# One decoder step on one core: weight passes in whole-row slabs over eight PSUM banks, residual by an identity product, cache pages over 8 partitions

## What is computed

```
mix = jnp.concatenate([rmsnorm(mla_o, w["norm_mla_out"]), gla_o], -1) @ w["w_out"]
h = x + mix
h = h + peer(rmsnorm(h, w["norm_ffn"]), w)
gate = jax.nn.sigmoid((rmsnorm(h, w["norm_ple"]) @ w["w_ple_gate"]).astype(F32)).astype(h.dtype)
return h + gate * (p_i @ w["w_ple_proj"])
```

## Time and profile before

| | |
|---|---|
| median of 3 runs | 5016.18 us |
| profiled execution, program time | 5022.3 us |
| profiled execution, span of the core | 5020.5 us |
| TensorE / VectorE / ScalarE / GpSimd busy | 46% / 68% / 10% / 47% |
| DMA queue 0 (gathers) / queue 1 (the other loads and stores) | 60.8% / 23.2% of 16 engines |
| moved | 1608.74 MB, mean 320 GB/s |

### The profile page before, as it was taken

One profiled execution on the slowest core, in us unless ns is written; L12 is line 12 of the kernel. 1 busy time (PEld: TensorE's weight loads), 2 busy tenths in 40 slices (PEclk: granted clock), 3 DMA queues, 4 the chain that ended last, 5 costly groups with the idle time before them and its releaser, 6 DMA issues.

```text
span 5020.5 us, 31657 instructions
## 1 busy us (share of the span) xinstructions
PE 2321.0 (46%) x10142; PEld 1769.8 (35%) x10142; DVE 3423.4 (68%) x3925; ACT 514.6 (10%) x1004; POOL 2342.1 (47%) x1172
## 2 busy tenths in 40 slices
PE   8565477642387348661655533566280000000735
PEld 7355367322276236431332222456270000000623
DVE  0227820988855980298777788558769999988583
ACT  1210100112100100110222211000100000000101
POOL 0001820663431260167565645441348888888361
PEclk9687689655598669865777766778595555555867
DMA  9267985998896496699899889986599999999996
GB/s 298 82 212 278 387 290 164 348 348 306 317 351 244 179 413 210 202 354 390 328 349 344 338 316 345 366 320 239 229 364 422 422 422 422 422 408 420 350 383 235
DMA packets 530150, 1608.74 MB, mean 320 GB/s; under 512 B 67637, under 2 KB 363574, under 8 KB 375081
## 3 DMA queue, kind: packets, MB, share of 16 engines
q0 software_dynamic: 167936, 1222.71, 60.8%
q1 hardware_dynamic: 351592, 375.58, 23.2%
q10 hardware_dynamic: 10496, 9.04, 0.5%
HBM read 1564.09 MB, written 42.56 MB: 320 GB/s over the span
## 4 chain that ended last, share of the span: by engine, by line
PE 31%; DVE 25%; DMA 14%; POOL 12%; SPq 8%; issue 6%; another core or an unknown queue 3%; ACT 2%; DVEq 0%; ACTq 0%; POOLq 0%
POOL ring L2088 12%; PE bank L734 11%; PE bank L727 11%; DVE total L1664 7%; DVE ring L1639 7%; SPq L558 5%; PE bank L1010 2%; DMA front<-in_w_in 2%; DMA front<-in_w_ple_gate 2%; DMA front<-in_w_out 2%; DMA front<-in_peer_w_q 1%; DMA ring<-in_peer_u,idx_all 1%; DMA xn_dram<-front 1%; DMA front<-in_cache_k_inv_rms 1%
## 5 line engine op out<-in xcount | busy, mean ns | idle before, releaser
L2088 POOL DMA_INDIRECT ring<-in_peer_u,idx_all x576 | 1173.0, 2037 | 1040.4 <-DVEq L1642 673.6
L2088 POOL DMA_INDIRECT ring<-in_peer_v,idx_all x576 | 1159.5, 2013 | 1047.4 <-DVEq L1667 572.7
L1664 DVE SCALAR_TENSOR_TENSOR total<-ring,gate_all,total 128x2048 f32<-128x2048 f32 x571 | 1341.9, 2350 | 92.6 <-DMA ring<-in_peer_v,idx_all 35.2
L1639 DVE CUSTOM_DVE_ANT_0 ring<-ring,xrow 128x2048 f32<-128x2048 f32 x576 | 1318.7, 2289 | 111.9 <-DVE dots L1639 60.8
L699 PE MATMUL bank<-ident,front 128*128 128x128 f32 (+1 forms) x320 | 67.9, 399 | 1452.1 <-DVE front L1099 1421.0
L734 PE MATMUL bank<-front 128*128 128x245 f32 (+3 forms) x2560 | 586.5, 386 | 111.9 <-DMA front<-in_w_in 83.4
L727 PE MATMUL bank<-front 128*128 128x245 f32 (+3 forms) x2560 | 590.2, 387 | 90.3 <-DMA front<-in_w_in 75.0
L699 PEld LDWEIGHTS bank<-ident,front 128*128 128x128 f32 (+1 forms) x320 | 54.6, 216 | 1466.0 <-DVE front L1099 1417.5
L734 PEld LDWEIGHTS bank<-front 128*128 128x128 f32 (+1 forms) x2560 | 470.4, 186 | 216.1 <-DMA front<-in_w_in 86.7
L727 PEld LDWEIGHTS bank<-front 128*128 128x128 f32 (+1 forms) x2560 | 471.4, 186 | 195.2 <-issue 110.6
L1138 DVE RECIPROCAL ms<-ms 128x1 f32<-128x1 f32 (+1 forms) x5 | 0.8, 162 | 535.7 <-ACT ms L1737 535.4
(11 more groups left out here) (283 smaller groups left out, 2650.0 us busy)
## 6 DMA issues: line engine op xcount, KB each, us to landing
front<-in_w_in SPq DMA_DIRECT2D x96, 980.0 KB, 6.1
front<-in_w_out SPq DMA_DIRECT2D x48, 1024.0 KB, 11.4
front<-in_peer_w_q SPq DMA_DIRECT2D x48, 1024.0 KB, 10.3
front<-in_w_ple_gate SPq DMA_DIRECT2D x48, 1024.0 KB, 10.0
front<-in_cache_kv_latent SPq DMA_DIRECT2D x128, 128.0 KB
front<-in_w_uq SPq DMA_DIRECT2D x6, 1536.0 KB, 9.8
ring<-in_peer_u,idx_all POOLq DMA_INDIRECT x576, 12.7
ring<-in_peer_v,idx_all POOLq DMA_INDIRECT x576, 10.8
```

The costliest lines, as they stand in the source:

```text
L1639: e.tensor_tensor_reduce(out=ring[:, b, :], in0=ring[:, b, :], in1=xrow[:, t % 2, :], scale=1.0, scalar=0.0, op0=ALU.mult, op1=ALU.add, ac ...
L1664: e.scalar_tensor_tensor(out=total, in0=ring[:, b, :], scalar=c1, in1=total, op0=ALU.mult, op1=ALU.add).then_inc(s("summed"), 1)
L2088: e.indirect_dma_start(out=ring[:, k % RING, :], out_offset=None, in_=a[("peer_u", "peer_v")[side]][0], in_offset=bass.IndirectOffsetOnAxi ...
```

## The change

- The weights come in slabs of 128 full rows. `slabs` on SyncE loads k-tile after k-tile into four buffers of 128 x 2048 (together as large as the two before). A slab of `w_in` is half of its columns (1960, two passes), of `w_out` and `w_ple_gate` all 2048; `w_ple_proj` follows as two more slabs. A slab of `peer_w_q` holds two k-tiles of half of the columns.
- `project` goes over k outermost: for each slab and tile four matmuls of 490 or 512 columns into four banks, so a group of two tiles fills all eight. Nothing can be emptied before the last slab. Then ScalarE copies the banks out: z to a 2-tile buffer and from there to DRAM in two stores per tile, the new residual to H, the sigmoid to Y and G, after which TensorE computes the embedding's projection into the same banks and VectorE multiplies and adds 512 columns at a time.
- The residual is added in PSUM: at k = 8 four matmuls with the identity bring H into the sum, and VectorE's additions go.
- The queries of all 8 heads of a half are summed side by side in 8 banks, copied, then the other half, and the key scores of all heads go into the banks after that. Ranking starts behind the last of them.
- A page of 128 tokens is laid over 8 partitions, 16 tokens in each: DRAM pieces of 16 KB, 4 KB and 512 bytes.
- The gains of the latent attention get a place of their own and are loaded once.
- `ROWS_BEFORE` and `STEPS_BEFORE` are new.

```diff
+            def slabs(name, w, col0=0, ncol=D, extra=None, between=None):
+
+                for k in range(KD + (PLE // P if extra is not None else 0)):
+                    n = PASSES[name] + k
+                    if k == SLABS and between is not None:
+                        between()
+                    if n >= SLABS:
+                        e.wait_ge(s("slabs_used"), n - SLABS + 1)
+                    src = w[k * P:(k + 1) * P, col0:col0 + ncol] if k < KD else extra[(k - KD) * P:(k - KD + 1) * P, :]
+                    e.dma_start(W[:, n % SLABS, 0:ncol], src).then_inc(s(f"w_landed{n % SLABS}"), 16)
...
-                                e.dma_start(dst[:, q, :], a[pool][0, bass.ds(pg, 1), :, :].rearrange("o p d -> (o p) d"))\
+                                e.dma_start(dst[q * 8:(q + 1) * 8, :, :],
+                                            a[pool][0, bass.ds(pg, 1), :, :].rearrange("o (r i) d -> (o r) i d", r=8))\
...
+            def project(name, use, tiles, ncol, freed=None, residual=False):
+
+                for k in range(KD):
+                    n = PASSES[name] + k
+                    transposed(use, tiles, k)
+                    e.wait_ge(s(f"w_landed{n % SLABS}"), 16 * (n // SLABS + 1))
+                    for sl, t in enumerate(tiles):
+                        R = ROWS[t]
+                        for c in range(4):
+                            if k == 0 and freed is not None:
+                                e.wait_ge(s("z_read"), freed + 4 * sl + c + 1)
+                            mm = e.matmul(bank[4 * sl + c][:R, 0:ncol], XT[:, k, sl * P:sl * P + R],
+                                          W[:, n % SLABS, c * ncol:(c + 1) * ncol], start=(k == 0), stop=(k == KD - 1))
+                    mm.then_inc(s("slabs_used"), 1)
+                    if residual and k == KD // 2:
+                        e.wait_ge(s("rows_loaded"), 16 * 3 * (tiles[-1] + 1))
...
+                            for c in range(4):
+                                e.matmul(bank[4 * sl + c][:R, :], ident[:R, :R], H[:R, sl, c * BANK:(c + 1) * BANK], start=False, stop=False)
...
+                for half in range(2):
                     for k in range(KD):
-                        mm = e.matmul(bank[side][:, 0:ntok], w[:, k, side * P:(side + 1) * P], XT[:, k, 0:ntok],
-                                      start=(k == 0), stop=(k == KD - 1))
-                    mm.then_inc(s("tiles_projected"), 1)
...
+                        for j in range(PH):
+                            if k == 0 and half:
+                                e.wait_ge(s("qT_evacuated"), 2 * PH * g + j + 1)
+                            at = (k % 2) * D // 2 + j * P
+                            mm = e.matmul(bank[j][:, 0:ntok], W[:, n % SLABS, at:at + P], XT[:, k, 0:ntok],
+                                          start=(k == 0), stop=(k == KD - 1))
...
+                for half in range(2):
+                    yield
+                    e.wait_ge(s("slabs_used"), PASSES[f"in{half}_{g}"] + KD)
+                    if half:
+                        e.wait_ge(s("z_stored0"), 16 * (tiles[-1] + 1))
+                    for sl, t in enumerate(tiles):
+                        R = ROWS[t]
+                        for c in range(4):
+                            e.copy(zst[:R, sl, c * IN_BANK:(c + 1) * IN_BANK], bank[4 * sl + c][:R, 0:IN_BANK]).then_inc(s("z_read"), 1)
...
 STEPS_BEFORE = [
-    36, 64, 132, 172, 219, 242, 262, 274, 328, 391, 442, 477, 504, 524, 570, 615, 655, 695, 714, 725, 737, 769, 815, 828,
-    828, 828, 828, 828, 828, 828, 828, 828, 828, 828, 846, 861]
+    11, 19, 21, 24, 64, 111, 124, 147, 188, 200, 202, 220, 252, 271, 291, 332, 366, 407, 441, 467, 482, 493, 504, 517,
+    528, 541, 542, 542, 542, 542, 542, 542, 542, 542, 555, 556]
```

More of the change, by code:

```diff
@@ L80 @@
 PASSES = {}
[L81 to L94, removed]
+_slabs = 0
+for _name, _n in ([(f"{k}{g}", n) for g in range(len(GROUPS))
+                   for k, n in (("in0_", KD), ("in1_", KD), ("out", KD), ("query0_", KD // 2), ("query1_", KD // 2))]
+                  + [(f"gate{g}", KD + PLE // P) for g in range(len(PLE_GROUPS))]):
+    PASSES[_name] = _slabs
+    _slabs += _n
 NORMS = {k: n for n, k in enumerate(
@@ L395, in first_slot @@
             return GATHERS.index((u, side)) * TOPK
[L397 to L401, removed]
-            else:
-                for i in range(lo, hi):
-                    yield i
         SSQ, RQ, IQ = ms[:, 0:1], ms[:, 1:2], ms[:, 2:3]
@@ new lines, in query_slabs @@
+            def query_slabs(g, half, between=None):
+                for i in range(KD // 2):
+                    if i == SLABS and between is not None:
+                        between()
+                    n = PASSES[f"query{half}_{g}"] + i
+                    e.wait_ge(s("slabs_used"), n - SLABS + 1)
+                    e.dma_start(W[:, n % SLABS, :].rearrange("p (k n) -> p k n", k=2),
+                                a["peer_w_q"][0][2 * i * P:(2 * i + 2) * P, half * D // 2:(half + 1) * D // 2]
+                                .rearrange("(k p) n -> p k n", p=P)).then_inc(s(f"w_landed{n % SLABS}"), 16)
@@ L615, in residual_rows @@
                     e.dma_start(G, down(a["norm_ffn"][0])).then_inc(s("gain_loaded"), 16)
-                weight_blocks(f"out{g}", a["w_out"][0], NC, NBLK, nt, between=residual_rows)
+                slabs(f"out{g}", a["w_out"][0], between=residual_rows)
                 def store_rows():
@@ L700, in norm_transposes, with transposed @@
                         mm.then_inc(s("nt_transposed"), 1)
-            def project(name, tiles, ncol, nblk, free, free0, embed=False):
-                nt = len(tiles)
-                landed = PASSES[name][0]
-                pg = int(name[-1])
-                with e.Fori(0, nblk // 2) as i:
-                    for p in range(2):
-                        w = W[p][:, 0:KD * ncol].rearrange("p (k n) -> p k n", k=KD)
-                        if embed:
-                            e.wait_ge(s(f"w_landed{p}_0"), i * 32 + (16 * landed + 16 * (landed - PASSES["gate0"][0]) + 32))
-                        else:
-                            e.wait_ge(s(f"w_landed{p}_0"), (i + landed + 1) * 16)
+            def transposed(use, tiles, k=None):
+                last = 4 * NORMS[use, tiles[-1]]
+                if len(tiles) > 1 and not k:
+                    e.wait_ge(s("nt_evacuated"), last + 4)
+                elif len(tiles) == 1 and k % 4 == 0:
+                    e.wait_ge(s("nt_evacuated"), last + k // 4 + 1)
@@ new lines, in embed @@
+            def embed(pg):
+                tiles = PLE_GROUPS[pg]
+                n0 = PASSES[f"gate{pg}"] + KD
+                for n in (n0, n0 + 1):
+                    e.wait_ge(s(f"w_landed{n % SLABS}"), 16 * (n // SLABS + 1))
+                for sl, t in enumerate(tiles):
+                    R = ROWS[t]
+                    for c in range(4):
+                        last = sl == len(tiles) - 1 and c == 3
+                        e.wait_ge(s("sigmoid_ready"), EMBEDDED[pg] + 4 * sl + c + 1)
+                        for k in range(PLE // P):
+                            mm = e.matmul(bank[4 * sl + c][:R, :], pT_ple[:, k, sl * P:sl * P + R],
+                                          W[:, (n0 + k) % SLABS, c * BANK:(c + 1) * BANK], start=(k == 0), stop=(k == 1))
+                            if last:
+                                mm.then_inc(s("slabs_used"), 1)
+                        if not last:
+                            mm.then_inc(s("embed_psum"), 1)
@@ L1067, in _ @@
                 e.wait_ge(s("pT_ple_sb"), done)
[L1068 to L1069 removed]
+                project(f"gate{pg}", "ple", tiles, BANK)
+                embed(pg)
         @block.vector
@@ L1129, in mixer @@
                 yield
-                for seg in range(IN_BLOCKS // 2 if g else 1):
-                    yield
-                e.wait_ge(s("mla_gains_loaded"), 64 * (g + 1))
+                e.wait_ge(s("mla_gains_loaded"), 64)
                 for t in tiles:
```

270 lines of the change are left out of this document (80 added, 190 removed), and 87 rows, old and new, of the table ROWS_BEFORE.

## The result

The changed kernel takes 5096.18 us, the median of 4 runs (5086.58 to 5116.17), against 5019.56 us for the kernel before in its 4 runs: a ratio of 1.016, 95% interval 1.0123 to 1.0197. It is 77 us slower. The forecast was 5095. That the sum met the time to within a few us is luck: two errors cancel, as the stages show.

A forecast was written before the change was run, and what follows sets the result against it. No engine was full (VectorE 68%, DMA queues about 85%), so time was read stage by stage: all routed 3876 + gathers 979 + hidden embeddings 156 + tail 90 = 5101 us span, stated as 5095, range 4895 to 5230.

The forecast's parts named there:

- The frame: Whole kernel: gathers run only for routed tiles; VectorE can take 240 before tile 1 is routed, 752 before tile 3.
- the slabs: Input passes of second and third groups: become TensorE's, 212 us plus 3 for emptying, against 308 and 320 us.
- the head start of the second group: Second group: latents at 835 us with 80 gathers, 30 us earlier and 12 gathers ahead.
- the slabs' half of 420 GB/s: Input pass: slab rows of 7.8 KB need 151 GB/s; the 8 KB gathers would leave them half of 420.
- The queries' order: All 16 queries before key scores: first gather 470 not 418 us (+52); second group's keys 1645, where the first came at 1535.
- The page term: Sample attention: page loads cost 36 us a group atop 22 gathers of 2.5 us, 91 us; eight groups 728 us.
- My own case: Whole kernel with page loads at 36 us a group: 5035 to 5175 us, chance 0.41.
- rival (b): Sample attention's page loads at quarter pace, 6.5 GB/s an engine: 52 us a group, 5229 us; chance 0.14.
- The mean DMA share falls, as eight engines idle: Sample attention, sign that the forecast is right: groups of 91 us with waits for gathers while mean DMA share falls.
- 16 KB pieces at over 1.5 us: Page loads, sign that the forecast is right: each 16 KB piece takes over 1.5 us.
- My upper bound of 100 us: Page loads: at 3.3 GB/s a partition, 8 partitions give 27 GB/s, 100 us a group.
- (a): Sample attention: page loads cost their bytes alone, 68 us a group, 4917 us, faster; chance 0.33.

The follow-up runs named there:

- run with cut slabs: Changed kernel with pages on 32 partitions 4 apart, each input-projection slab loaded by eight DMAs of 245 columns (980-byte pieces): 5025.37 us, ratio 1.001.
- runs with early keys: Changed kernel, key scores of heads 0 to 3 behind first query half: old pages 4818.54 us; 32 partitions 4 apart, ScalarE's second-half copies behind routes, 4696.35 us.

## Why the forecast came out right, and which step failed

**The frame and the slabs held.** The pass took 214 us (forecast 215), the latents came 20 us early (12 of them are a slip in my sum: 798 + 25 is 823, not 835), and the cap of 240 (all that VectorE can take before tile 1 is routed) made the head start of the second group worthless: VectorE did 9 us of work between 1341 and 1608 us. The run with cut slabs shows the mechanism, the length of a piece. What I called the slabs' half of 420 GB/s is a share by pieces, and equal only because the pieces are nearly equal.

**The queries' order held.** First gather 463 (+45, forecast +52), keys of the second group 1609. The runs with early keys give that back: 4779 to 4696, 83 us. After the first keys I was too dear: ranking and routes up to the next loads took 152 us where I wrote 178. Some 14 of that is a slip again, as 140 us and ten gathers of 2.4 us make 164.

**The page term is the step that failed.** I took 36 us a sequence, the geometric middle of 12.8 and 100. It was (911 - 211 x 2.5) / 8 = 48: the stage 393 to 604 took 911 us and not 822, 89 more. What hid it: the stages up to gather 393 came 56 us early (2270 for 2326), and those behind the linear attention 47 us (1632 from gather 681 to the end, forecast 1679). 89 - 56 - 47 is -14, the difference of the two spans. My own case stood at 91 us a sequence; 103 is nearer to rival (b), quarter pace, with 52 us a group. It is nearest to the estimate by the Trainium skill, "SBUF — State Buffer", section "Door 1: The DMA port swizzle": two ports, 50 us a group. By (b) the sum came to 5229 only because my other stages were too dear as well; with the measured 48 us it would have been 5197. The luck reaches further than the match of 5095 and 5096: had the sample attention taken my 822 us and all else what it took, the time would have been 5096 - 89 = 5007, no slower than the kernel before. So the direction, too, came out right by the page term's being worse than I said.

**The signs that I named for it were wrong.** "The mean DMA share falls, as eight engines idle": it stayed at 0.96 to 1.02. "16 KB pieces at over 1.5 us": 1.15 us on average. The engines read as busy while little moves; the sign is GB/s at a full share. My upper bound of 100 us took a page load alone; beside gathers one took 72 us (2492.6 to 2564.6) and cost 48, as gathers go on at half pace. That a 64-partition store among gathers lost nothing drew me toward (a); but it was 1.5 us long, and 64 partitions reach eight groups, not two. Against (a) I also wrote that SyncE issues a page every 1.6 us; that is the pace of single issues in the slowest load before (77 us for 48), three to a page, and the changed kernel issued sixteen pages in 36 us (2489.3 to 2525.4), 2.3 us each.

**The parts add up, but only nearly.** Whole rows are worth 246 us (5025 to 4779), the queries' order costs 83, the page layout 240: 5017 - 246 + 83 + 240 = 5094, for 5096 measured. The 246 is too much for the kernel before, though: its two late input passes took 308 and 320 us, those of the run with cut slabs 339 and 349, 60 us more. With 186 the sum is 5154. So some 60 us of gain are not assigned; identity product, emptying and the new table are in them, and no run took these apart.

## What to carry to other kernels

When one change has several parts, forecast each stage with its own clock and count, and compare those, not the sum: here +89 and -103 gave a span that was only 14 us off. A load that is small in bytes can be dear by its place: beside a stream that needs every DMA engine, spread each of its DMAs over all parts of the memory (here 32 partitions 4 apart instead of 8 neighbours, 317 us), and don't cut it much shorter than the stream's pieces, or it will be starved instead: pieces of 4 KB came in time here, those of 1 KB late in all three layouts. Before computing all of something in one pass, see who waits for its first part.

## What the runs showed of the hardware

- A page load into 8 neighbouring partitions halved the pace of gathers that write all 128: 13.9 for 25.9 GB/s per busy engine, with all engines busy. By groups reached, 2, 4, 8, 16 groups cost 41, 28, 12 and 1 us a sequence of 2.69 MB above 62, with pieces of 4 or 16 KB.
- Two queues with work shared the engines piece for piece: 4635 packets each in 92 us, of 8 KB in one and 980 bytes in the other. So weight pieces of 980 bytes beside gathers of 8 KB got 1 MB in 22.8 us; in rows of 7.8 KB the same buffers and order got 1 MB in 6.7 us, at TensorE's pace.
- A load in 1 KB pieces into 8 partitions 16 apart moved 49 GB/s with nothing beside it, at the pace of SyncE's issues (a page every 3.65 us).
